# Four of twelve modulation slices move from TensorE's row products to sums on GpSimd

## What is computed

```python
silu_c  = jax.nn.silu(c)                                  # [1, 1024]
silu_cc = jax.nn.silu(c_ctx)                              # [1024]
mod_l = (silu_c  @ mod_w + mod_b).reshape(1, 6, 1, 1024)  # six vectors for the tokens
mod_c = (silu_cc @ mod_w + mod_b).reshape(6, 1, 1024)     # six for the context tokens
h_lat = modulate(rms_norm(lat, norm_g[0]), mod_l[:, 0], mod_l[:, 1])
h_ctx = modulate(rms_norm(cx,  norm_g[0]), mod_c[0],    mod_c[1])
y_lat, y_ctx = gla_mixer(h_lat, h_ctx, ...)               # gated linear attention
lat = lat + mod_l[:, 2] * rms_norm(y_lat, norm_g[1])
h   = modulate(rms_norm(lat, norm_g[2]), mod_l[:, 3], mod_l[:, 4])
lat = lat + mod_l[:, 5] * rms_norm(swiglu(h, ffn_w_in, ffn_w_out), norm_g[3])
```

## Time and profile before

| | us |
|---|---|
| three runs | 1214.74, 1212.92, 1214.64 |
| median | 1214.64 |
| the profiled execution | 1214.05 |
| its span in the trace | 1212.3 |
| busy in the span: TensorE | 1164.5 (96%) |
| VectorE | 724.4 (60%) |
| ScalarE | 557.8 (46%) |
| GpSimd | 55.6 (5%) |

### The profile page before, as it was taken

The page is one execution under the profiler, slowest core; times in us unless marked ns, Lnnn a source line. Parts: engine busy times, 40 slices in busy tenths (PEclk is TensorE's granted clock), DMA queues, the critical chain, the costliest instruction groups (busy, mean ns, idle before and its releaser), DMA issues.

```text
span 1212.3 us, 19101 instructions
## 1 busy us (share of the span) xinstructions
PE 1164.5 (96%) x7496; PEld 1007.3 (83%) x7500; DVE 724.4 (60%) x1049; ACT 557.8 (46%) x762; POOL 55.6 (5%) x63
## 2 busy tenths in 40 slices
PE   5889998899999999999999999999999999999997
PEld 2477785599999988647999999999999988999996
DVE  2778336464555476655465456666677776654653
ACT  3562332443334362644244246666666665433432
POOL 1000042000000070000000000000000000000000
PEclk9999999999999989999999999999999999999999
DMA  9764362898655550617645634555555434746500
GB/s 352 234 241 166 125 257 62 291 276 255 198 171 160 157 160 1 222 57 249 209 170 198 228 107 114 147 157 156 156 156 142 138 132 162 275 176 208 184 24 35
DMA packets 201057, 209.41 MB, mean 173 GB/s; under 512 B 5819, under 2 KB 166982, under 8 KB 200806
## 3 DMA queue, kind: packets, MB, share of 16 engines
q1 hardware_dynamic: 198576, 201.61, 52.4%
q0 software_dynamic: 1648, 4.83, 1.5%
q10 hardware_dynamic: 774, 2.17, 0.5%
HBM read 207.53 MB, written 2.01 MB: 173 GB/s over the span
## 4 chain that ended last, share of the span: by engine, by line
PE 88%; DMA 4%; DVE 2%; ACT 2%; SPq 2%; issue 1%; ACTq 0%; DVEq 0%
PE bank L2070 22%; PE bank L2072 22%; PE bank L2071 22%; PE bank L2342 2%; PE bank L1894 2%; PE bank L1895 2%; PE bank L1896 2%; DMA weight_pool<-in_mod_w_dram 2%; SPq L473 2%; DMA weight_pool<-in_gla_w_in_dram 1%; PE bank L1834 1%; PE bank L2469 1%; PE bank L2454 1%; PE bank L2445 1%; PE bank L2479 1%; DMA normed<-in_ctx_dram 1%
## 5 line engine op out<-in xcount | busy, mean ns | idle before, releaser
L2070 PE MATMUL bank<-hT_high,mlp_up_high 128*128 128x256 f32 x512 | 145.2, 284 | 0.9 <-DVE hT_low L1480 0.9
L2071 PE MATMUL bank<-hT_low,mlp_up_high 128*128 128x256 f32 x512 | 144.9, 283 | 0.0
L2072 PE MATMUL bank<-hT_high,mlp_up_low 128*128 128x256 f32 x512 | 144.9, 283 | 0.0
L2070 PE MATMUL bank<-od_w_high,hT_high 128*128 128x384 f32 x376 | 130.1, 346 | 0.0
L2072 PE MATMUL bank<-od_w_high,hT_low 128*128 128x384 f32 x376 | 126.1, 335 | 0.0
L2071 PE MATMUL bank<-od_w_low,hT_high 128*128 128x384 f32 x376 | 125.8, 335 | 0.0
L1141 DVE TENSOR_TENSOR mlp_down_low<-weight_pool,mlp_down_high 128x2048 fp32r<-128x2048 f32 x32 | 73.3, 2289 | 59.0 <-ACT mlp_down_high L662 59.0
L1141 DVE TENSOR_TENSOR od_w_low<-weight_pool,od_w_high 128x3072 fp32r<-128x3072 f32 x24 | 80.5, 3356 | 41.1 <-ACT od_w_high L662 41.1
L2070 PEld LDWEIGHTS bank<-hT_high,mlp_up_high 128*128 128x128 f32 x512 | 98.1, 192 | 2.8 <-issue 1.9
L2070 PE MATMUL bank<-mlp_down_high,hidden_high 128*128 128x512 f32 x256 | 99.9, 390 | 0.0
L2071 PE MATMUL bank<-mlp_down_low,hidden_high 128*128 128x512 f32 x256 | 99.9, 390 | 0.0
(11 more groups left out here) (362 smaller groups left out, 2631.4 us busy)
## 6 DMA issues: line engine op xcount, KB each, us to landing
weight_pool<-in_mlp_w_dram SPq DMA_DIRECT2D x64, 1024.0 KB, 7.7
weight_pool<-in_od_w_in_dram SPq DMA_DIRECT2D x72, 512.0 KB, 5.3
weight_pool<-in_mod_w_dram SPq DMA_DIRECT2D x22, 1024.0 KB, 9.8
weight_pool<-in_ffn_w_in_dram SPq DMA_DIRECT2D x44, 512.0 KB, 5.5
weight_pool<-in_gla_w_in_dram SPq DMA_DIRECT2D x12, 1024.0 KB, 5.9
weight_pool<-in_ffn_w_out_dram SPq DMA_DIRECT2D x22, 512.0 KB, 6.6
weight_pool<-in_gla_w_out_dram SPq DMA_DIRECT2D x2, 2048.0 KB, 14.2
weight_pool<-in_ev_w_in_dram SPq DMA_DIRECT2D x4, 1024.0 KB, 6.7
```

The lines of the kernel that those rows point to most:

```text
L2070: mm(out_, left[0], right[0], start=start, stop=False, **flag)
L2071: mm(out_, left[0], right[1], start=False, stop=False, **flag)
L2072: return mm(out_, left[1], right[0], start=False, stop=stop, **flag)
```

## The change

Slices 4, 5, 10 and 11 leave TensorE's list, ScalarE's copies, VectorE's reductions and SyncE's loads. GpSimd fetches them itself, a row block of 128x512 at a time (256 KB), into two halves of `normed`, multiplies a block by its column of `silc` spread along the row, and adds it to the slice's sum row, the other half of `normed`; a block's buffer is fetched again when both are done. TensorE then multiplies the sum row by a column of ones, four matmuls of 128x128 by one column, which adds over the partitions and turns the row in one (`mod_column`); VectorE adds the bias. Slices 4 and 5 are summed behind the first chunk's high part, and their columns stand behind the last projection; 10 and 11 are summed behind the first gate row, once the second norm's tokens are turned, and their columns stand before the 19th step of the feed-forward layer. Slices 6 and 7 write their copies to a tile of their own (`late_row`).

```diff
-LATE_AFTER = {0: (4,), 1: (5,), 5: (6,), 7: (7,)}
+LATE_AFTER = {5: (6,), 7: (7,)}
+ROW_SLICES = (0, 1, 2, 3, 6, 7, 8, 9)
+SUM_SLICES = (4, 5, 10, 11)
+SLICE_ORDER = (0, 1, 2, 3, 6, 7, 4, 5, 8, 9, 10, 11)
...
+        def sum_row(i):
+
+            return normed[:, 1024 + 512 * (i % 2):1536 + 512 * (i % 2)]
...
-            sp.wait_ge(s["og_ready"], 2)
-            sp.dma_start(view(work, 16384, KD, 512), mod_v[:, :, 10, :]).then_inc(s["mod_loaded"], 16)
-            for half in range(2):
-                fetch(L["mod", 11, half])
...
+            def sums_fetch(n):
+
+                i, k = SUM_SLICES[n // KD], n % KD
+                g.dma_start(normed[:, 512 * (n % 2):512 * (n % 2) + 512], mod_v[:, k, i, :]).then_inc(s[f"sums_in{n % 2}"], 16)
+
+            def mod_sums(first, slices):
+
+                last = first + KD * slices
+                for n in range(first, first + 2):
+                    sums_fetch(n)
+                for n in range(first, last):
+                    i, k, w = SUM_SLICES[n // KD], n % KD, normed[:, 512 * (n % 2):512 * (n % 2) + 512]
+                    done = 2 * n - n // KD
+                    factor = silc[:, k, 0:1].to_broadcast([P, 512])
+                    g.wait_ge(s[f"sums_in{n % 2}"], 16 * (n // 2) + 16)
+                    g.tensor_tensor(w if k else sum_row(i), w, factor, ALU.mult).then_inc(s["mod_sums"], 1)
+                    if k:
+                        g.wait_ge(s["mod_sums"], done)
+                        g.tensor_tensor(sum_row(i), sum_row(i), w, ALU.add).then_inc(s["mod_sums"], 1)
+                    if n + 2 < last:
+                        g.wait_ge(s["mod_sums"], done + 1)
+                        sums_fetch(n + 2)
+
+            g.wait_ge(s["silu_done"], 2)
+            g.wait_ge(s["xT_ps"], 4)
+            mod_sums(0, 2)
             g.wait_ge(s["ke_ready"], 2)
             g.wait_ge(s["kd_ready"], 4)
             g.memset(work[:, 12288:14336], 0.0).then_inc(s["pool_zeroed"], 1)
...
             gate_rows(0)
+            g.wait_ge(s["xT_ps"], 12)
+            mod_sums(2 * KD, 2)
             gate_rows(1)
...
             def late_stats(t):
 
                 y_stats(0, t)
-                if t:
-                    mod_copy(10)
-                    mod_copy(11)
...
+            def mod_column(i):
+
+                if i == 4:
+                    pe.wait_ge(s["dve_init"], 2)
+                pe.wait_ge(s["mod_sums"], 15 * SUM_SLICES.index(i) + 15)
+                pe.wait_ge(s["mod_cols"], slice_place(i) - 2)
+                for c in range(4):
+                    ins = mm(slice_bank(i, 1)[:, c:c + 1], sum_row(i)[:, P * c:P * c + P], stat[:, 176:177], start=True, stop=True)
                 ins.then_inc(s["mod_turned"], 1)
...
             for i in turn_next:
                 mod_turn(i)
+            mod_column(4)
+            mod_column(5)
             pe.wait_ge(s["silu_r"], 4)
...
             ins.then_inc(s["out_used"], 1)
-            mod_slice(10)
-            mod_slice(11)
-            mod_turn(10)
-            mod_turn(11)
             turn_tokens(2, xn)
...
+            mod_column(10)
+            mod_column(11)
             ffn_round(FF_LOOPS * FF_RING, FFC - FF_LOOPS * FF_RING, last=True)
```

More of the change, by code:

```diff
@@ L203, in slice_rows, with slice_count, slice_place @@
             at = 512 * (i % 2)
-            return work[:, 4096 + at:4608 + at] if i < 4 else xn[:, 0, at:at + 512] if i < 8 else hTs[:, at:at + 512]
+            return work[:, 4096 + at:4608 + at] if i < 4 else late_row[:, :] if i < 8 else hTs[:, at:at + 512]
+        def slice_count(i):
+            return ROW_SLICES.index(i) + 1
+        def slice_place(i):
+            return SLICE_ORDER.index(i) + 1
+        def sum_row(i):
+            return normed[:, 1024 + 512 * (i % 2):1536 + 512 * (i % 2)]
         def slice_bank(i, turned):
@@ L346, in ring_slice @@
             for half in range(2):
-                ring_chunk(("mod", i, half), (4, 512), mod_v[:, 4 * half:4 * half + 4, i, :], ("mod_rows", i + 1))
+                ring_chunk(("mod", i, half), (4, 512), mod_v[:, 4 * half:4 * half + 4, i, :], ("mod_rows", slice_count(i)))
         def ring_weights(c):
@@ L368, in program @@
                 L["mod", i, half] = plan(f"mod{i}_{half}", 4096 * (i - 8) + 2048 * half,
-                                         [(0, (4, 512), mod_v[:, 4 * half:4 * half + 4, i, :])], ("mod_rows", i + 1),
+                                         [(0, (4, 512), mod_v[:, 4 * half:4 * half + 4, i, :])], ("mod_rows", slice_count(i)),
                                          ring=f"w_ring{2 * (i - 8) + half}")
@@ L1096, in _ @@
             dve.memset(stat[:, 90:91], EPS).then_inc(s["dve_init"], 1)
+            dve.memset(stat[:, 176:177], 1.0).then_inc(s["dve_init"], 1)
             dve.wait_ge(s["vec_ps"], 1)
@@ L1146, in low_weights @@
                 low(pair[1][:, :], pool[:, e.at + off:e.at + off + pair[1].shape[1]], pair[0][:, :], done)
+            def mod_column(i):
+                dve.wait_ge(s["mod_turned"], slice_place(i))
+                dve.tensor_tensor(mods[:, 4 * i:4 * i + 4, 0], slice_bank(i, 1)[:, 0:4], vecA[:, VA_MB + 4 * i:VA_MB + 4 * i + 4], ALU.add)\
+                   .then_inc(s["mod_cols"], 1)
             def mod_reduce(i):
-                dve.wait_ge(s["mod_turned"], i + 1)
+                dve.wait_ge(s["mod_turned"], slice_place(i))
                 v = slice_bank(i, 1)[:, :].rearrange("p (c g q) -> p c q g", c=4, g=4)[:, :, 0:2, :]
@@ L1310, in _ @@
             gate_logs(1)
-            mod_reduce(5)
             proj(6)
```

43 lines of the change are left out of this document (16 added, 27 removed).

## The result

The changed kernel takes 1224.45 us (median of 4 runs), the one before 1213.78 on the same chip: a ratio of 1.0088, interval 1.0072 to 1.0104. That is 10.7 us slower. The profiled execution of after has a span of 1222.5 us against 1212.3.

A forecast was written before the change was run, and what follows sets the result against it. TensorE was taken to bound most of the kernel, with gapless VectorE equally limiting chunks 2 to 6. Chunk 6's +8.75, then +1.9 + 1.2 - 4.6 + 1.9 + 0.5, made +9.65 us on 1214.05; 1224 was said, range 1217 to 1229.

The forecast's parts named there:

- VectorE's lead: Projections, GpSimd's disturbance left out: earlier gate logarithms and fewer reductions bring the copy freeing chunk 6's first bank 7.2 us earlier.
- The turns: VectorE's gapless projections stretch: GpSimd gets 14 whole-instruction turns of 1.28 us on the shared SBUF ports, adding 17.9 us.
- The rule of the Trainium skill: VectorE's gate logarithms: if two-port tensor-scalar instructions also take the port lock, 2.6 us more, 1226.3; not in the sum.
- The slow start: Chunk 6 in the projections: TensorE works slower after idling, +1.9 us (bounds 0.9 and 3).
- The columns: TensorE's one-column matmuls ending each slice: +1.2 us behind the last projection, +1.9 in the feed-forward layer.
- third rival: Projections: GpSimd's transfers land late, so TensorE waits at the one-column matmuls; 1233 or 1261 us, chance 0.09.
- Before the layer: Stretch ahead of the feed-forward layer: without slices 10 and 11 ScalarE's square begins earlier, -4.6 us (bounds -4.1 and -4.8).
- The lock in the layer: First third of the feed-forward layer: a GpSimd turn can fall on VectorE's first split, which TensorE awaits; +0.5 us.
- first rival: Projections: GpSimd gets no turn between VectorE instructions that follow each other at once; 1206 us, chance 0.28.
- the sum without GpSimd: Whole kernel if GpSimd took no turns from VectorE: -7.2 + 1.2 - 4.6 + 1.9 = -8.7 us, or 1206.

The follow-up runs named there:

- small sums: Changed kernel, but GpSimd's sums of slices 4 and 5 touch only 8 of 512 columns, transfers and waits kept: 1205.18 us, ratio 0.9935 to the kernel before.
- second profile of before: The kernel before, unchanged, profiled once more on the chip of the other experiments: 1213.11 us (one run).
- one other version: Changed kernel, but GpSimd stops after two row blocks of slice 4 until VectorE has made the decayed keys and queries: 1208.70 us, ratio 0.9962 to before.
- the tensor-scalar multiply: Changed kernel, but GpSimd multiplies by a tensor-scalar instruction with silc's column as per-partition scalar: 1210.82 us, ratio 0.9990 to the kernel before.

## Why the prediction was right

1224 was said, with a range of its own from 1217 to 1229, and 1224.45 measured; by the profiled executions +9.65 us was said and +10.2 measured. Term by term:

- **VectorE's lead, -7.2.** Right within 0.6 us as a term of its own: with small sums the copy that frees chunk 6's first bank starts at 101.67 instead of 109.46, 7.8 earlier, and the gate logarithms' first input comes at 62.68 instead of 69.94, 7.3 earlier. In the changed kernel this input comes at 65.65, only 4.3 earlier. The prediction counted turns only from the logarithms on; the subtraction for chunk 1 (3.63 us at 53.50) and the second absolute value (3.37 at 57.05) lie before, and took turns too. Mis-sized by 3 where GpSimd works.
- **The turns, 14 x 1.28 = 17.9.** Fourteen of the fifteen two-operand instructions other than the scans are longer, by 0.43 to 1.24, together 13.3 us; the subtraction at 99.83 is not. The two small copies behind the scans add 1.5, the tensor-scalar 0.8, the scans 0.4: 16.1. So seventeen instructions took a turn instead of fourteen, and a turn cost 0.95 us instead of 1.28, since a multiply by a broadcast column takes 1.05 alone, and since a turn can fall in part on a VectorE instruction that reads only PSUM: the subtraction at 85.57 lost 0.43, as GpSimd's add had begun beside the one from PSUM at 84.91. The mechanism is the predicted one. But that chunk 6, said for 120.8, began at 121.80 is luck in part: 3 us too much of lead and 1.8 too much of turns nearly cancel.
- **The rule of the Trainium skill.** The Trainium skill (SBUF — State Buffer, "Who interferes with whom") has tensor-scalar instructions in a two-port form in the lock as well. The trace agrees: 2.06 us at 88.20 against 1.23 in the earlier trace rows, and 1.51 for the first. That is 1.1 us of the 2.6 that the prediction would have added for it.
- **The slow start, +1.9.** Chunk 6 took 13.8 us (121.80 to 135.59) instead of 11.2: +2.6. Between 120 and 140 the granted clock was 0.83; in the version with small sums, where TensorE has no gap ahead of chunk 6 (105.47), it was 1.00 between 100 and 120, and chunk 6 took 11.2. The two stretches, changed kernel first:

```profile
120.00:140.00 20.00, 18.20 (x71) 14.87 (x72) 11.42 (x11) 1.92 (x1) 8.49 (x4) 0.83 0.45 160
```

```profile
100.00:120.00 20.00, 20.00 (x99) 15.14 (x98) 10.26 (x11) 4.34 (x3) 3.92 (x6) 1.00 0.60 201
```

- **The columns, +1.2 and +1.9.** +0.9 and +1.8. The sums ended at 129.8, not 155: transfers landed in 4.1 us and turns cost GpSimd less. The third rival needed 177.
- **Before the layer, -4.6.** The turn came 4.7 earlier against all else, but took 1.97 instead of 1.09 behind an idle 4.30, with the granted clock at 0.50, the lower of its two levels, from 247.0 to 249.2, and the gap gained 4.3. Against the second profile of before, with its gap of 13.50, it is 3.3.
- **The lock in the layer, +0.5.** 0 in the profile; 0.3 of waiting in one other version.
- **Behind the layer, no term.** -0.7: the stretch to the next projections takes 16.53 us instead of 17.23. It differs by 0.4 between the two profiles of before as well.

The first rival, GpSimd gets no turns, had 1206 as its price. The version with small sums, in which the turns cost VectorE nothing, took 1205.18: the sum without GpSimd was right to 1 us. With the tensor-scalar multiply part of that rival came true: multiplies that wait while VectorE keeps its length.

## What to carry to other kernels

Work moved to an idle engine is free only if it does not take turns with an engine that is on the path: look for two-operand VectorE instructions without a gap, count them, and take a turn of the other engine for each. If the work has slack, put it where the busy engine idles; a wait on a point that the busy engine passes is enough, and a form of instruction that costs the other engine less of a turn helps as well. A gain of a few us read from segments of one trace has to be held against the spread between executions, which here was as large.

## What was not expected of the hardware

GpSimd's tensor-scalar instruction of 128x512 takes 1.55 us alone, half as long again as the tensor-tensor form with a broadcast column (1.05), and at 54.27 waited through two VectorE instructions, where the tensor-tensor form was served after one (the add at 78.72). A tensor-tensor instruction of 8 columns waits too: it took 1.9 to 3.9 us behind VectorE's subtractions and scans, with 0.20 for itself:

```profile
67.43 3.85 POOL L572 TENSOR_TENSOR normed<-normed,silc 128x8 f32<-128x8 f32 x1
```

VectorE's copy of 128x32 out of SBUF, 0.19 us, took 1.07 beside GpSimd's add (75.68), so a short copy waits for a whole instruction of the other as well.
